# Seven block products in all four feed-forwards: products added on VectorE, weight sums on GpSimd, picks counted 1.3 times in the plan, x loaded by tiles

## Reference

```python
def conv_ffn(h, hist, w_up, w_conv, b_conv, w_down):
    a, gate = jnp.split(h @ w_up, 2, axis=-1)          # w_up: 1024 x 5632
    ext = jnp.concatenate([hist.astype(a.dtype), a], axis=1)
    conv = b_conv
    for j in range(CONV_W):                             # 3
        conv = conv + ext[:, j:j + t] * w_conv[j]
    return (jax.nn.silu(conv) * gate) @ w_down, ext[:, t:]
```

## Time and profile before

| | |
|---|---|
| median of 3 runs | 4004.64 us (4002.97 to 4010.16) |
| profiled execution | 4004.88 us |
| its span, first to last instruction | 4003.0 us |
| PE busy | 3717.8 us (93%) |
| DVE busy | 2334.5 us (58%) |
| ACT busy | 1125.3 us (28%) |
| POOL busy | 758.4 us (19%) |
| DMA, mean | 85 GB/s |

### The profile page before, as it was taken

How to read it: one execution, slowest core, us unless ns; L and a number is a source line. 1 busy time by engine, 2 the same in 40 slices (tenths; PEclk the granted TensorE clock), 3 DMA queues, 4 the chain that set the end, 5 groups by cost and what they waited for, 6 DMA issues and landing times. The chain is left out here.

```text
span 4003.0 us, 54393 instructions
## 1 busy us (share of the span) xinstructions
PE 3717.8 (93%) x21676; PEld 2953.6 (74%) x21676; DVE 2334.5 (58%) x4713; ACT 1125.3 (28%) x2668; POOL 758.4 (19%) x812
## 2 busy tenths in 40 slices
PE   7978899999999999999899989999899999899998
PEld 5755678777877777777667877787767777688887
DVE  1663556599964553549546454289955655544542
ACT  1123333211134442321334233111134443312221
POOL 2200121201001032221000014313010001353344
PEclk9988899999999999999999999999999999899999
DMA  4322233412222132342221213333221122242223
GB/s 141 96 76 75 81 98 89 129 67 70 79 67 68 51 96 93 90 124 89 62 91 54 80 59 96 115 110 122 70 69 52 42 75 69 70 149 83 65 89 96
DMA packets 152757, 339.54 MB, mean 85 GB/s; under 512 B 30312, under 2 KB 70824, under 8 KB 139192
## 3 DMA queue, kind: packets, MB, share of 16 engines
q1 hardware_dynamic: 92728, 291.04, 23.3%
q10 hardware_dynamic: 59776, 45.02, 3.9%
HBM read 299.33 MB, written 36.68 MB: 84 GB/s over the span
## 5 line engine op out<-in xcount | busy, mean ns | idle before, releaser
L835 PE MATMUL PS<-xn,wring 128*128 128x272 f32 (+1 forms) x7168 | 1709.1, 398 | 73.1 <-ACT dense L1163 29.2
L835 PEld LDWEIGHTS PS<-xn,wring 128*128 128x128 f32 x7168 | 1387.1, 196 | 348.1 <-issue 48.7
L1776 POOL TENSOR_TENSOR xT<-xT,res 128x272 f32<-128x272 f32 (+1 forms) x320 | 252.6, 790 | 2391.9 <-ACT res L1118 2356.6
L835 PE MATMUL PS<-dense,wring 128*128 128x256 f32 (+1 forms) x2816 | 666.1, 395 | 17.8 <-DVE dense L1436 9.2
L835 PEld LDWEIGHTS PS<-dense,wring 128*128 128x128 f32 x2816 | 541.6, 195 | 118.4 <-issue 10.7
L1545 DVE MAX8 top<-scr 128x8 f32<-128x384 f32 (+6 forms) x418 | 367.4, 879 | 12.5
L1546 DVE MATCH_REPLACE8 scr<-top,scr 128x384 f32<-128x384 f32 (+6 forms) x418 | 359.8, 861 | 0.0
L1118 ACT ACTIVATE res<-PS 128x272 f32<-128x272 f32 (+1 forms) x320 | 123.9, 389 | 600.5 <-PE PS L835 576.4
L856 PE MATMUL PS<-wring,xn 128*128 128x256 f32 (+1 forms) x1152 | 266.0, 391 | 3.7 <-ACT dense L1132 3.7
L856 PEld LDWEIGHTS PS<-wring,xn 128*128 128x128 f32 (+1 forms) x1152 | 213.3, 187 | 50.0 <-ACT dense L1132 5.4
L835 PE MATMUL PS<-catT,wring 128*128 128x272 f32 (+1 forms) x1024 | 231.1, 387 | 2.5 <-DVE catT L1615 1.8
(11 more groups left out here) (196 smaller groups left out, 4127.5 us busy)
## 6 DMA issues: line engine op xcount, KB each, us to landing
wring<-in_wu SPq DMA_DIRECT2D x88, 1024.0 KB, 4.8
wring<-in_wf SPq DMA_DIRECT2D x88, 512.0 KB, 3.8
wring<-in_wo SPq DMA_DIRECT2D x64, 512.0 KB, 3.7
wring<-in_wd SPq DMA_DIRECT2D x96, 320.0 KB, 2.9
wring<-in_wd SPq DMA_DIRECT2D x64, 384.0 KB, 3.1
wring<-in_wn SPq DMA_DIRECT2D x16, 1024.0 KB, 5.4
kv<-out_projT ACTq DMA_DIRECT2D x48, 256.0 KB, 4.1
out_projT<-dense SPq DMA_DIRECT2D x40, 272.0 KB
```

Source lines behind the costliest of these rows:

```text
L835: mm = nc.tensor.matmul(PS[:, dbank(t.g0), 0:cw], wtile(t.q, i), rhs, start=(kk == a), stop=(kk == b - 1))
L1776: nc.gpsimd.tensor_tensor(x, x, res[:, i % NRES, 0:cw], ALU.add).then_inc(s_res, 1)
```

## The change

- Blocks 2 to 21 of F00, F01 and F10 become seven block products too (60 more blocks); F11 keeps its 20.
- The mixer still uses `kv`, `scr` and `bias` there, so the buffers move: T2, T3, T4 and the partial products lie in x of the *other* half, T1 in place of B12 in `xn`, S1 and S4 in the weight tile, S3 in `inv`, S2 in a new `wsum`. x of the other half is written to DRAM (in `yT`) six turns into P10 and P11 and read back ten turns after a feed-forward's last branch turn (after F00 from the input, since it has not changed).
- P7 is moved ahead of P5. POOL makes S4 after P2, and S3, S2, S1 of the next block after P7 and at P3, where it made all four in one row. ACT's copies of P1, P6 and P7 wait for the sums on DVE of the block before.
- T2 to T4 are made right after the norm's second scaling. T1 waits for the last direct block.
- `step_times` counts a pick 1.3 times as long as before.
- x of h = 0 is loaded in 8 transfers of 544 columns (there were 16 of 272). The first norm of P01 is no longer made in P00 but at the start of P01.

```diff
+SEVEN = {(0, 0): range(2, NF), (0, 1): range(2, NF), (1, 0): range(2, NF), (1, 1): range(1, NF - 1)}
-PRODUCTS = (Product("P1", "A11", "B11"), Product("P2", "A12", "B21"), Product("P6", "S2", "T2"), Product("P5", "S1", "T1"),
-            Product("P7", "S3", "T3"), Product("P3", "S4", "B22"), Product("P4", "A22", "T4"))
+PRODUCTS = (Product("P1", "A11", "B11"), Product("P2", "A12", "B21"), Product("P6", "S2", "T2"), Product("P7", "S3", "T3"),
+            Product("P5", "S1", "T1"), Product("P3", "S4", "B22"), Product("P4", "A22", "T4"))
+S_ORDER, T_ORDER = ("S3", "S2", "S1", "S4"), ("T3", "T2", "T4", "T1")
+U_ORDER = ("U2", "a0", "U3", "P5 + P3", "a1", "g0", "g1")
...
-    if l == 0 and h == 0:
+    if l == 0:
         _norm(l, h, 0, 0, 1)
-    elif l == 0:
-        _turn("nsc", l, h, 0, 1, 0, ng=0)
...
-        if (l, h, g) == (0, 0, "c"):
-
-            for j in range(2):
-                _root(0, 1, 0, j, 1)
...
-                out.append((0, 0, min(BURST, ROUNDS[h][y] - BURST * z) * 2 * (1.04 * k + 0.15), 0))
+                out.append((0, 0, min(BURST, ROUNDS[h][y] - BURST * z) * 2.6 * (1.04 * k + 0.15), 0))
...
         res = sb("res", [P, NRES, GMAX])
+        wsum = sb("wsum", [P, 4 * P])
...
+        def add_products(lane, eng, t):
+            (c0, cw), (c1, _) = GRP[t.h]
+            a, g, fixed = ab[:, t.n % 2, :], gb[:, t.n % 2, :], len(U_ORDER) * BLOCKS.index((t.l, t.h, t.n))
+            g0, g1 = g[:, c0:c0 + cw], g[:, c1:c1 + cw]
+            p1, u2, u3 = (part_of(t, i) for i in range(3))
+            name = PRODUCTS[t.p].name
+            def into_a(c, x, x0):
+                for b, w, gap in a_cols(t, c, cw):
+                    here = a[:, gap + b:gap + b + w]
+                    ins = eng.tensor_tensor(here, here, x[:, x0 + b - c:x0 + b - c + w], ALU.add)
+                ins.then_inc(s_fix, 1)
+            if name in ("P6", "P7", "P3", "P4"):
+                lane.wait_ge(s_ea, t.g0 + 1)
+            if name == "P6":
+                eng.tensor_tensor(u2, u2, p1, ALU.add).then_inc(s_fix, 1)
+                into_a(c0, p1, 0)
+            elif name == "P7":
+                lane.wait_ge(s_fix, fixed + 1)
+                eng.tensor_tensor(u3, u3, u2, ALU.add).then_inc(s_fix, 1)
+            elif name == "P3":
+                into_a(c1, g, c1)
+                lane.wait_ge(s_fix, fixed + 4)
+                into_a(c1, u2, 0)
+            elif name == "P4":
+                lane.wait_ge(s_fix, fixed + 4)
+                eng.tensor_tensor(g0, g0, u3, ALU.add).then_inc(s_fix, 1)
+                eng.tensor_tensor(g1, g1, u3, ALU.add).then_inc(s_fix, 1)
+        def tanh_turn(t, l, h, n):
+            k = UP_END[l, h, n]
+            return k + (3 if t.kind == "s" else 2 if TURNS[k].kind == "s" and t.p < 3 else 1)
+        def product_turn(t, l, h, n):
+            return tanh_turn(t, l, h, n) + (t.kind != "dn")
...
+            if name in ("S2", "S3"):
+                return wsum[:] if name == "S2" else inv[:, 0:4 * P]
+            a = {"A11": 0, "A12": 512, "S4": 512, "A21": 1024, "S1": 1024, "A22": 1536}[name]
...
+            if name in ("T2", "T3", "T4") or name == "T1" and (l, h) == (1, 1):
+                a = 4 * cw * (int(name[1]) - 2)
+                flat = scr[:, 0:4 * cw] if name == "T1" else x_all[1 - h][:, a:a + 4 * cw]
+                return flat.rearrange("p (k t) -> p k t", k=4)
...
+            cw = GRP[t.h][0][1]
+            return x_all[1 - t.h][:, (12 + i) * cw:(13 + i) * cw]
...
             sp.eng.dma_start(mean[:], io["mean"]).then_inc(s_mean, 16)
             for k in range(KD):
-                sp.eng.dma_start(xT[:, k, 0:GMAX], io["xT"][k * P:(k + 1) * P, 0:GMAX]).then_inc(s_x[0][k], 16)
+                sp.eng.dma_start(x_of[0][:, k, :], io["xT"][k * P:(k + 1) * P, 0:W[0]]).then_inc(s_x[0][k], 16)
...
+            def put_aside(l, h):
+                z = max(k for k, t in enumerate(TURNS) if t.kind == "dn" and (t.l, t.h) == PROJS[PROJS.index((l, h)) - 1])
+                sp.wait_ge(s_res, ADDS[z] + 1)
+                sp.eng.dma_start(x_kept(1 - h), x_of[1 - h]).then_inc(s_aside, 16)
...
+            def load_again(l, h):
+                sp.wait_ge(s_mm, TURNS[UP_END[l, h, NF - 1]].g0 + 1)
+                sp.wait_ge(s_fix, len(U_ORDER) * sum(1 for x in BLOCKS if x[0:2] <= (l, h)))
+                src = x_kept(1 - h) if (l, h) in ASIDE else io["xT"].rearrange("(k p) t -> p k t", p=P)[:, :, C0[1 - h]:C0[1 - h] + W[1 - h]]
+                sp.eng.dma_start(x_of[1 - h], src).then_inc(s_back, 16)
...
+                for l, h in ASIDE:
+                    if k == STAGE[{(0, 1): "P10", (1, 0): "P11"}[l, h]][0] + 6:
+                        put_aside(l, h)
+                for l, h in BACK:
+                    if k == UP_END[l, h, NF - 1] + 10:
+                        load_again(l, h)
...
-                    if nextq == 0:
-                        for kk in range(KD):
-                            sp.eng.dma_start(xT[:, kk, GMAX:W[0]], io["xT"][kk * P:(kk + 1) * P, GMAX:W[0]]).then_inc(s_x[0][kk], 16)
...
+                    if name in ("P1", "P6", "P7"):
+                        act.wait_ge(s_xs, 4 * list(SEVEN).index((t.l, t.h)) + 1)
+                        act.wait_ge(s_fix, max(0, len(U_ORDER) * (B - 1) + {"P1": 2, "P6": 5, "P7": 7}[name]))
+                    else:
+                        act.wait_ge(s_h, max(0, U - 1))
...
+                    if (t.l, t.h) in SEVEN and (t.n, t.j) == (1, 1):
+                        b = lambda name: x_block(t.l, t.h, name)
+                        n0 = 4 * list(SEVEN).index((t.l, t.h))
+                        if (t.l, t.h) in ASIDE:
+                            dve.wait_ge(s_aside, 16 * (ASIDE.index((t.l, t.h)) + 1))
+                        dve.wait_ge(s_xn, KD * (SCALES.index(k) + 1))
+                        nc.vector.tensor_tensor(b("T3"), b("B22"), b("B12"), ALU.subtract).then_inc(s_xs, 1)
+                        dve.wait_ge(s_xs, n0 + 1)
+                        nc.vector.tensor_tensor(b("T2"), b("T3"), b("B11"), ALU.add).then_inc(s_xs, 1)
+                        dve.wait_ge(s_xs, n0 + 2)
+                        nc.vector.tensor_tensor(b("T4"), b("B21"), b("T2"), ALU.subtract).then_inc(s_xs, 1)
                 if t.kind == "s" and t.p == 0 and t.n == SEVEN[t.l, t.h][0]:
...
+                    if (t.l, t.h) == (1, 1):
+                        dve.wait_ge(s_ct, NPAIR * 4)
+                    else:
+                        dve.wait_ge(s_mm, t.g0)
                     nc.vector.tensor_tensor(b("T1"), b("B12"), b("B11"), ALU.subtract).then_inc(s_xs, 1)
...
+            def first_sums(B):
+                k = LAST[("s",) + BLOCKS[B] + (0,)]
+                weights_in(pool, TURNS[k].q)
+                pool.wait_ge(s_xn, KD * (norm_of(k) + 1))
+                if B:
+                    pool.wait_ge(s_mm, group_of(B - 1, "P7") + 1)
+                weight_sum(B, "S3", "A11", "A21", ALU.subtract)
+                weight_sum(B, "S2", "A22", "S3", ALU.subtract)
+                next_block = BLOCK_Q.get(t.q + 1)
+                if t.kind == "s":
+                    name = PRODUCTS[t.p].name
+                    if (t.l, t.h) in ON_POOL:
+                        add_products(pool, nc.gpsimd, t)
+                    if name == "P2":
+                        pool.wait_ge(s_mm, t.g0 + 1)
+                        weight_sum(BLOCK_Q[t.q], "S4", "A12", "S2", ALU.subtract)
+                    elif name == "P7" and next_block is not None:
+                        first_sums(next_block)
+                    elif name == "P3" and next_block is not None:
+                        weight_sum(next_block, "S1", "A21", "A22", ALU.add)
+                elif next_block is not None and k == FIRST_OF[t.q]:
+                    first_sums(next_block)
+                    weight_sum(next_block, "S1", "A21", "A22", ALU.add)
+                if (t.kind, t.n, t.p, t.j) == ("wo", 0, 0, 0) and PROJS.index((t.l, t.h)):
+                    pool.wait_ge(s_back, 16 * sum(1 for x in BACK if x < (t.l, t.h)))
                 if t.kind in ("wo", "dn"):
```

More of the change, by code:

```diff
@@ L501, in build @@
         neglam = sb("neglam", [P, L])
-        xT, xn = sb("xT", [P, KD, T]), sb("xn", [P, KD, WMAX])
+        xT, xn = sb("xT", [P, KD * T]), sb("xn", [P, KD, WMAX])
         catT = sb("catT", [P, KD, WMAX])
@@ L634, in scaled_of, with a_cols @@
+        def a_cols(t, c, cw):
+            if c + cw <= HALF:
+                return ((c, cw, 2),)
+            return ((c, HALF - c, 2), (HALF, c + cw - HALF, 4))
         def scaled_of(k):
@@ L1097, in dense_scalar @@
             for k, t in enumerate(TURNS):
-                if pending is not None and k > UP_END[pending[0:3]] + (2 if t.kind == "s" else TURNS[UP_END[pending[0:3]]].kind == "s"):
+                if pending is not None and k >= tanh_turn(t, *pending[0:3]):
                     l, h, n, U = pending
@@ L1440, in dense_vector @@
             for k, t in enumerate(TURNS):
```

(2 more changed lines are left out.)

135 lines of the change are left out of this document (47 added, 88 removed).

## The result

The changed kernel takes **4070.3 us** (median of 3 runs, 4068.3 to 4071.7) where the kernel before takes 4004.6. The recorded ratio is 1.0146, with a 95% interval of 1.0123 to 1.017; the quotient of the two medians, 1.0164, lies within it. By the medians the change costs 66 us, by the ratio 59; 23 were forecast. The profiled execution took 4071.7 us, its span is 4069.9.

A forecast was written before the change was run, and what follows sets the result against it. Bound by PE outside the picks, by DVE or both inside them. F00 and P10 +30, F01 -6, F10 with P11 +2, start -4, P01's norm +5, F11 -4: +23 on 4004.9, 4028 us; eight in ten 3950 to 4090.

The forecast's parts named there:

- The wait beside POOL: In direct blocks, DVE's two-input instructions wait while POOL makes weight sums: 1.8 us a block, bounds nothing and 2.4.
- DVE's added work: In F00, F01 and F10, sums and waits of 5.1 or 4.8 us a block, plus 4 a feed-forward for T.
- The window of F00's picks: F00's first blocks up to its last pick: DVE gets 418 us of work, so 438 us where 329 were.
- the sign I had named: In the window of F00's picks, DVE at 95% or more and PE under 85% would show the steps right.
- F10 with P11: First branch stretch +9, `dn` stretch behind it -29 of PE time, later turns +3 and waiting 18: +2 us in all.
- x as a transfer: Two stores and three loads of x, 2 MB each, taken as hidden; some 13 us each if unhidden.
- catches up in the `dn` stretch: DVE, maybe a block behind when a branch stretch ends, catches up in `dn`: 15 us back in F00, F01 and F10.
- it is PE that counts there: Behind F00's last pick PE sets the pace (95% busy), so its 64 us less work shorten that stretch by 64.
- The waiting of "4%" in the later stretches: In F01's and F10's later stretches PE waits more often for busier DVE: 17 us and 18 us.
- The start with P00 and P01: Fewer SP transfers at the start -4; P01's norm now in the open, partly offset by P00, +5.
- The sums fit: Rival, 0.27: weight sums hardly meet DVE (0.4 us a block) and finer waits cost nothing, 3954 us.
- The third case: Rival, 0.23: DVE bounds attention and recurrence stretches too, with F11's 2.4 us and 8% waiting, 4080 us.

The follow-up runs named there:

- a2: The changed kernel with POOL's four weight sums a block cut to 2 columns, all waits kept: 3981.2 us (0.9931).
- a7: The changed kernel with every pass of a pick run over 64 keys only: 3896.2 us (0.9731).
- a12: The changed kernel with sums of products and of weights cut to 2 columns and pick passes over 64 keys, all instructions and waits kept: 3826.8 us (0.9541).

## Why the forecast was too small

**Right.** The mechanism and the sign: PE spared, DVE given more, the picks stretch longer. The rows spared (480; but they are worth 91 to 99 us of PE's time at full clock, not 108, and PE's busy time fell by 57, not by about 100). The price of a sum, 0.42 to 0.44 us undisturbed. The wait beside POOL, taken as 1.8 us a block between 0 and 2.4: 2.1. DVE's added work, 312 us by my prices (40 x 5.1, 20 x 4.8, 12 for the T): 312 outside F11, and 294 with the 17 us that F11 has less. So the load on DVE was right, and what failed is the step from load to time. The window of F00's picks, forecast at 438 us: 437 (though DVE was busy 403 us of it, 92%, not 418 and 95%; two errors that cancel, and the sign I had named, 95% or more, was missed). Its last pass starts at 1232.95 us, by a forecast of about 1240. F10 with P11, forecast +2: 0, although the stretches in it came out otherwise. F11, at most -4: -4.5. x as a transfer was hidden: PE's waits for a DMA are two of the mixer's, 2.9 us in all.

**The step that failed: "catches up in the `dn` stretch".** I took 15 us off for F00, F01 and F10 each. In F01's first branch stretch I forecast 149 us, less 15; measured were 150.1. The stretches behind it were forecast at +5 together and came at +7. So of F01's miss, +13 for -6, 16 us are this term. In F00 and P10 the window of the picks came as forecast without it, and the window behind the last pick was to be 64 us shorter, or 79 with the 15; it became 40 shorter. So the 15 are not there. In F10 the term is missing too, but that is hidden: its first branch stretch took 154.6 us for a forecast of 159, since DVE had only 148.8 us of work there, not 169. At the forecast's 97% these 148.8 make 153 us, with nothing taken off.

The trace shows why there was so little to catch up. The end of F01's first branch stretch: the first rows of `dn` on PE, and the last step of block 7's convolution on DVE:
```profile
2021.42 7.93 PE L901 MATMUL PS<-dense,wring 128*128 128x256 f32 x36
...
2023.91 0.75 DVE L1569 SCALAR_TENSOR_TENSOR dense<-dense,par 128x512 f32<-128x512 f32 x1
```
DVE ends the last convolution 3.3 us behind PE's last product. At the same places in F00 and F10 it is 8.9 and 10.4 us behind, where the kernel before has 5.2 and 3.3; a block takes PE some 13. At none of the three was DVE a block behind: PE had already waited for it inside the stretch (in F01's it was idle for 32 us, 15 before). The window of F00's first `dn` stretch shows besides that DVE has no room there:
```profile
942.00:997.00 55.00, 47.96 (x200) 38.15 (x199) 50.56 (x78) 8.40 (x19) 14.95 (x17) 0.94 0.30 94
```
DVE is at 92% there too, since passes fill it.

**A second step: "it is PE that counts there".** Behind F00's last pick another 24 us are missing. Of the 64 us that PE was to have less, it had 50.5; the low clock took 11 of the difference (24.3 us lost, 13.6 before). And PE's idle time rose from 27.5 to 38.0 us, where I had it unchanged.

**The term that was absent: the granted clock.** I priced waits by their own length. PE lost 34 us more to the low clock, 29 of them in F00 and 11 in F01 (all other stages together -6). Beside 127 us of idle time that is a fifth of what PE lost. Not all of it is in the miss: 19 of F00's 29 lie in the window of the picks, where DVE sets the pace and the length came as forecast.

**The waiting of "4%" in the later stretches** was about right: idle time outside the first stretch rose by 15 us in F01 (+17 forecast) and by 24 in F10 (+18). The start with P00 and P01 came out at -10 for my +1, a miss to the other side that hid 11 us of the first two.

**My rivals.** "The sums fit" (3954) falls with a2: it needed 0.4 us a block beside POOL, and there were 2.1. Even with that wait all but gone, a2 takes 3981. The third case, DVE as bound in the later stretches too, has the nearest time (4080), but not by its mechanism: it had 8% of waiting there, and PE's idle share rose by 3 points in F01 (7.4 to 10.2%) and by 4 in F10 (5.4 to 9.5%). What it has right is that sums cost outside the picks: a7 less a12 shows 69 us from them where the passes are short. I priced sums and passes as loads that add up; they cost 69 and 86 us singly, 243 together.

## To carry to other kernels

When work moves from the busiest engine to the second, price it where the second is already full, and again for what a stall of the first costs: here 127 us of idle PE came with 34 us lost to the low clock. Don't count on a late engine catching up: look in the trace how far behind it is at the end of a stretch, and whether the window behind has room. Split a mixed change: one number of the plan was worth 38 us of gain, and hid under the 125 us that the block products cost. And when a queue looks like the cause, move it alone: here the wait only moved to the next copies.
